# Row products dealt out between the sample tokens' selection operations, and U's blocks fetched three ahead of V in the last stage

## The reference, cut to what matters

```python
q = (xt @ w_q)                               # 8 heads, two halves of 128
s1, s2 = (halves of q against 128 sub-keys each)
v1, i1 = top_k(s1, 16);  v2, i2 = top_k(s2, 16)
cand = v1[:, None] + v2[None, :]             # 16 x 16 pairs a head
top_s, pos = top_k(cand, 16);  idx = i1 * 128 + i2 at pos
g = softmax(top_s)
act = gelu(u_tab[idx] . x)                   # 128 experts a token
out = sum(g * act * v_tab[idx])              # tables of 16384 x 1024
```

## Time and profile before

| | us |
|---|---|
| median of three timed runs | 2609.61 (2608.39 to 2610.11) |
| profiled execution, its own time | 2614.08 |
| its span, first to last instruction | 2612.3 |
| PE busy | 2377.7 (91% of the span) |
| DVE busy | 1766.5 (68%) |
| POOL busy | 908.3 (35%) |
| ACT busy | 777.9 (30%) |

### The profile page before, as it was taken

How to read it: one execution, slowest core, us unless ns; L and a number is a source line. 1 busy time by engine, 2 the same in 40 slices (tenths; PEclk the granted TensorE clock), 3 DMA queues, 4 the chain that set the end, 5 groups by cost and what they waited for, 6 DMA issues and landing times.

```text
span 2612.3 us, 34126 instructions
## 1 busy us (share of the span) xinstructions
PE 2377.7 (91%) x12686; PEld 1830.0 (70%) x12686; DVE 1766.5 (68%) x3612; ACT 777.9 (30%) x1388; POOL 908.3 (35%) x650
## 2 busy tenths in 40 slices
PE   5988899969999999999978778998899999999995
PEld 4756689859757766666657567987795777666662
DVE  1345479978668777677754456897884886777775
ACT  2354442113225422122243444311231452222221
POOL 3400360431221154555444205217113114555552
PEclk7999989989999999999989888999899999999997
DMA  6455334886799899999934702279669998999993
GB/s 262 139 179 193 131 112 129 312 313 226 281 316 317 281 366 370 366 364 366 366 115 147 209 25 85 92 269 360 207 223 344 313 320 316 377 378 356 384 369 133
DMA packets 219907, 679.71 MB, mean 260 GB/s; under 512 B 32384, under 2 KB 63152, under 8 KB 219232
## 3 DMA queue, kind: packets, MB, share of 16 engines
q1 hardware_dynamic: 142912, 396.42, 43.2%
q0 software_dynamic: 76832, 281.11, 28.7%
HBM read 658.87 MB, written 18.56 MB: 259 GB/s over the span
## 4 chain that ended last, share of the span: by engine, by line
PE 60%; DVE 15%; DMA 13%; ACT 4%; issue 3%; POOL 3%; SPq 1%; ACTq 0%; DVEq 0%
PE ps L1056 15%; PE ps L737 9%; PE ps L739 9%; PE ps L738 9%; DMA ring<-in_u 8%; PE ps L1033 7%; DVE arena L2033 3%; POOL arena L655 3%; PE ps L1012 2%; PE ps L919 2%; DMA arena<-gelu_half 2%; DMA arena<-in_u_rows,arena 2%; PE ps L900 2%; DVE arena L1927 1%; ACT u_split L1324 1%
## 5 line engine op out<-in xcount | busy, mean ns | idle before, releaser
L1056 PE MATMUL ps<-ring,arena 128*128 128x512 f32 x1264 | 568.9, 595 | 20.7 <-DVE arena L1981 20.6
L655 POOL DMA_INDIRECT arena<-in_u_rows,arena x256 | 294.0, 1148 | 782.6 <-DVE arena L2014 598.3
L655 POOL DMA_INDIRECT arena<-in_v,arena x256 | 355.8, 1390 | 353.8 <-DVE arena L2014 168.3
L1033 PE MATMUL ps<-arena,ring 128*128 128x256 f32 x2048 | 457.6, 382 | 1.1 <-ACT arena L1279 0.6
L1033 PEld LDWEIGHTS ps<-arena,ring 128*128 128x128 f32 x2048 | 386.5, 191 | 53.2 <-issue 1.9
L1056 PEld LDWEIGHTS ps<-ring,arena 128*128 128x128 f32 x1264 | 231.4, 190 | 268.8 <-issue 268.2
L615 POOL TENSOR_TENSOR ring_lo<-ring,ring_hi 128x1024 fp32r<-128x1024 f32 x84 | 216.4, 2588 | 415.5 <-ACT ring_hi L1158 415.5
L2014 DVE CUSTOM_DVE_ANT_0 arena<-arena 128x1024 f32<-128x1024 f32 x256 | 310.8, 1221 | 47.9 <-DMA arena<-in_u_rows,arena 47.5
L2033 DVE SCALAR_TENSOR_TENSOR arena<-arena 128x1024 f32<-128x1024 f32 x254 | 325.7, 1282 | 15.3 <-DMA arena<-in_v,arena 1.2
L737 PE MATMUL ps<-xs_high,u_split 128*128 128x256 f32 x1024 | 335.4, 328 | 0.1
L2003 DVE TENSOR_TENSOR u_split<-ring,u_split 128x1024 fp32r<-128x1024 f32 x128 | 156.7, 1224 | 218.4 <-ACT u_split L1324 218.4
(11 more groups left out here) (245 smaller groups left out, 3549.1 us busy)
## 6 DMA issues: line engine op xcount, KB each, us to landing
ring<-in_u SPq DMA_DIRECT2D x256, 512.0 KB, 6.3
ring<-in_v SPq DMA_DIRECT2D x256, 512.0 KB, 5.9
ring<-in_w_mod SPq DMA_DIRECT2D x80, 512.0 KB, 4.2
ring<-in_w_in SPq DMA_DIRECT2D x36, 512.0 KB, 3.3
ring<-in_w_q SPq DMA_DIRECT2D x32, 512.0 KB, 3.2
gelu_half<-arena SPq DMA_DIRECT2D x120, 128.0 KB, 4.7
arena<-gelu_half SPq DMA_DIRECT2D x120, 128.0 KB, 4.7
arena<-in_w_mod SPq DMA_DIRECT2D x16, 512.0 KB, 19.8
```

The costliest lines, as they stand in the source:

```text
L655: pool.indirect_dma_start(row[at], None, table, bass.IndirectOffsetOnAxis(where[:, k:k + 1], axis=0)).then_inc(sem(f"row_in{at}"), 16)
L1033: ins = mm(hidden_bank(b), slot[c % RING][:, P * k:P * k + P], HFS[:, k, :], start=(k == 0), stop=(k == KC - 1))
L1056: ins = mm(ps[:, t + 3 * q, :], GL[:, b % GLS, P * t - P:P * t], slot[c % RING][:, 512 * q:512 * q + 512], start=(b == MIDDLE[0]), stop=(b ...
```

## The change

```diff
-PICKED = 26
-PLAIN = 36
+PICKED = 37
+PLAIN = 39
-EARLY_DOTS = FIRST_DOTS + 20
-MIDDLE_DOTS = 38
+EARLY_DOTS = FIRST_DOTS + 16
+MIDDLE_DOTS = 42
...
         def u_chunk(l, b):
-            return c0 + b if b < SPILL else c0 + 128 + b - SPILL if b < SPILL + 2 else c0 + 130 + 2 * (b - SPILL - 2)
+            return c0 + b if b < SPILL else c0 + 128 + b - SPILL if b < SPILL + 3 else c0 + 131 + 2 * (b - SPILL - 3)
         def v_chunk(l, b):
-            return c0 + SPILL + (b + GLS) % SPILL if b < SPILL else min(c0 + 131 + 2 * (b - SPILL), c0 + KEYS + b)
+            return c0 + SPILL + (b + GLS) % SPILL if b < SPILL else min(c0 + 132 + 2 * (b - SPILL), c0 + KEYS + b)
...
-                    if b == 20:
+                    if b == 28:
                         exponents(1, P, STOK)
...
             def retrieve(l):
+                first_dots = iter(range(FIRST_DOTS))
+                def next_dot():
+                    for k in first_dots:
+                        dot(l, k)
+                        return True
...
-                def top16(pieces):
+                def top16(pieces, beside=False):
                     for s, v, x in pieces:
                         ins = dve.max(v[:, 0:8], s)
                     link(ins)
-                    for s, v, x in pieces:
+                    for n, (s, v, x) in enumerate(pieces):
                         ins = dve.max_index(x[:, 0:8], v[:, 0:8], s)
+                        if beside and n % 4 == 3:
+                            next_dot()
...
                     top16([(C[:, t, h, 0:CANDS], TV[:, t, h, :], TP[:, t, h, :])
-                           for t in range(first, last) for h in range(HEADS)])
+                           for t in range(first, last) for h in range(HEADS)], first > 0)
...
+                            if t:
+                                next_dot()
...
                 gates(1, 1, NT, ar(Q_ID + 7 * P, STOK)).then_inc(sem("picked"), 1)
+                while next_dot():
+                    pass
...
-                dots = 0
-                while dots < FIRST_DOTS:
-                    dot(dots)
-                    dots += 1
+                dots = FIRST_DOTS
```

More of the change, by code:

```diff
@@ L1833, in attention, with row_in, dot @@
                         mod_columns(MOD_STAGES[mods[0]][0] + (mods[1] + 2 * n - 6) // 4)
-            def retrieve(l):
+            def row_in(l, r):
+                n = PLACE[r]
+                dve.wait_ge(sem(f"row_in{row_slot[n]}"), 16 * row_turn(l, n))
+                return row[row_slot[n]]
+            def dot(l, k):
+                x = row_in(l, k)
+                dve.tensor_tensor_reduce(x, x, HP, 1.0, 0.0, ALU.mult, ALU.add,
+                                         HSEL[:, k:k + 1]).then_inc(sem("row_used"), 1)
+            def retrieve(l):
+                first_dots = iter(range(FIRST_DOTS))
[3 more added lines that the diff above has]
+                        return True
                 S = ar(Q_S, NT * 2048).rearrange("p (t c n) -> p t c n", t=NT, c=16)
@@ L2003, in low_u @@
                     tt(u_half(b, 1), slot[c % RING], f32(u_half(b, 0)), ALU.subtract).then_inc(used(c % RING), 1)
[L2005 to L2015, removed]
                 def dots_done(r):
@@ L2028, in accumulate @@
                 def accumulate(k):
-                    x = row_in(P + k)
+                    x = row_in(l, P + k)
                     if k:
@@ L2046, in experts @@
                     while dots < FIRST_DOTS + (EARLY_DOTS - FIRST_DOTS) * p // (PIECES - 1):
-                        dot(dots)
+                        dot(l, dots)
                         dots += 1
@@ L2079, in experts @@
                     for k in late_dots:
-                        dot(k)
+                        dot(l, k)
                     for k in late_sums:
```

## The result

The changed kernel takes 2546.3 us (median of four runs, 2539.5 to 2547.9) where the kernel before, run beside it, takes 2609.0: a ratio of 0.976, 95% interval 0.974 to 0.978, 62.7 us less. The forecast was 2560, its range 2538 to 2580. The profiled execution after is the fastest of the four, and that of before lay above its median, so the two profiles differ by more, 74.6 us of span. I therefore read the gain stage by stage. Here is the page of the changed kernel: the span and the groups of the two lines of PE that the change aimed at (busy us, mean ns, then the idle time in front and what ended most of it).

The account below looks back on a forecast made before the run. PE works nearly all of the mixer, so only its standing still could give time back. -32.6 + 2 - 19 = -49.6 took 2614.1 to 2564.5, less 4.5 to the median: 2560 us, range 2538 to 2580.

Parts of the forecast that it names:

- The hidden stage: Both layers' hidden stages: dealing products into the selection and picking later gives -32.6 us, bounds -22 to -50.
- U late from 486 to 537: Hidden stage beside dense gathers: 51 us in which 12.2 blocks of U arrive where PE could do 14.8.
- A starvation of 8.8 us a layer: Hidden stage: PE loses 8.8 us waiting for U beside the gathers, bounds 0 and 14.
- The first build at 563.6: Hidden stage: first one-hot build moves from 569.1 to 554.8 without new waits, to 563.6 with U late.
- the 127.6 us: Hidden stage behind the first build: 32 builds and 27 blocks in the old trace; 117.2 with three blocks moved ahead.
- The last stage: Last stages: U requested one pace of 6.30 us earlier removes PE's waits, -19 us, bounds 0 and -24.
- One of my marks: Last stage: sign to look for in the changed profile, U landing no sooner than now.
- The middle stage: Middle stages: four more products a layer cost +2 us, bounds 0 and 9.2 for both layers.
- rival 1: Hidden stage: U is not starved beside the gathers, gaining 17.6 us more, 2542 us; chance 0.17.
- Rival 2: Last stage is bound by bytes, giving back 17 of the 19 us, 2577 us; chance 0.15.
- Rival 3: Hidden stage: late rows push `picked` past block 37 and PE waits; 10 us a layer, 2580 us; chance 0.06.
- Rival 4: Last stage: V behind U(b + 3) in SP's queue, late in all 128 steps; at 0.5 us each, 2643; chance 0.05.

Follow-up runs that it names:

- e5: Changed kernel with only the first quarter of each of U's blocks 12 to 45 fetched in the hidden stage (computes something else); 2525.4 us, ratio 0.969.
- e2: Changed kernel with U fetched two ahead again, leaving only the products' part of the change; 2570.3 us, ratio 0.987 to the kernel before.
- e7: Changed kernel with 20 products among the builds and 38 in the middle stage instead of 16 and 42; 2538.5 us, ratio 0.975.
- e1: Kernel before with only U fetched three ahead; 2575.1 us, ratio 0.989.

## Why the prediction was right, and where it was off

**The hidden stage: -32.6 predicted, -35.6 in the profiles.** Its steps held to within a microsecond or two; in each pair here the first number is the prediction's. `picked` at 532.4: 532.55. The last product at 543.8: 543.9. U late from 486 to 537 at 4.17 us a block: from 487 to 533, mostly at 4.09 (491.82 to 495.91) and at 4.19 on average (eleven blocks from 487.13 to 533.23). A starvation of 8.8 us a layer: e5, which lifts it, gives 8.8 and 9.0. The first build at 563.6: 561.66, after a start that was 1.8 us earlier. The order of the queues was told rightly as well: U comes after 12.8 us where it was asked for 10.4 ahead. The missing 1.6 and 1.4 us a layer lie behind the first build. There I took the 127.6 us from the trace of before unchanged. But PE began them straight after a wait: this is the kernel before at the end of the wait, at the first build and after it (window, PE and PEld busy, DVE, ACT, POOL, granted clock, DMA share, GB/s).

```profile
541.00:569.00 28.00, 3.94 (x18) 2.96 (x16) 20.35 (x35) 0.77 (x2) 7.80 (x8) 0.63 0.90 361
569.00:571.00 2.00, 1.89 (x17) 1.89 (x18) 2.00 (x5) 0.00 (x0) 0.00 (x0) 0.50 0.00 0
571.00:575.00 4.00, 4.00 (x19) 3.41 (x19) 4.00 (x7) 1.08 (x2) 0.00 (x0) 0.88 0.00 0
```

The changed kernel at its first build:

```profile
560.00:566.00 6.00, 6.00 (x41) 5.37 (x40) 3.14 (x5) 1.47 (x3) 0.00 (x0) 1.00 0.60 199
```

Before, the granted clock is 0.50, 1.2 GHz, on the first build, which took 1.93 us there and 1.16 in the changed kernel, where it is 1.00; around the block behind it, it is 0.88 (4.22 against 3.67 us). So 1.3 of the 127.6 us, which I used for both layers, went with the wait. In layer 1 of the kernel before the same two took 1.93 and 5.58 us, 2.7 more than in the changed kernel.

**The last stage: -19 predicted, -29.7 measured.** This is the term of the sum that was mis-sized, and most of the 13.7 us between the forecast and the median. I set the gain nearly equal to the 20.7 us of listed waits and the bound at -24, which the measurement passes. The stage's whole length says more. Layer 0's last stage in the kernel before:

```profile
902.00:1314.00 412.00, 400.09 (x1978) 273.45 (x1978) 290.81 (x320) 85.73 (x127) 208.13 (x155) 1.00 0.95 356
```

and in the changed kernel:

```profile
876.00:1271.00 395.00, 395.00 (x1980) 272.67 (x1979) 293.26 (x321) 83.11 (x127) 208.32 (x155) 1.00 0.97 371
```

PE's busy time for the same instructions fell by 5.1 us, beside 11.9 us of listed waits: 17.0 of the 17.3. Most of it is not the clock, which has a mean of 1.00 in both. One wait of e2 tells it closely. It is listed as 0.97 us, but the `outer` behind it starts 1.13 us later than at the matmuls' pitch of 0.12 us, because the last matmul in front counts as busy for 0.28 us, to its end. The step from that `outer` to the next then takes 6.38 us and not 6.31. That makes 0.23 us beyond the list, about 5.5 us if all 24 waits are like it.

Another 1.7 us is the clock after all, in a stretch too short to show in the mean. It stands behind the longest wait of layer 0 in the kernel before (a row of PE's timeline, then a window as above):

```profile
1120.18 5.37 PE L1056 MATMUL ps<-ring,arena 128*128 128x512 f32 x8 [2.74 <-DVE arena L1981]
...
1121.60:1124.90 3.30, 3.30 (x5) 1.33 (x4) 3.20 (x4) 0.77 (x1) 2.34 (x3) 0.50 0.89 278
```

With the granted clock at 0.50 for most of it, the eight matmuls took 5.37 us and not 3.60, and the step to the next `outer` 8.07. e2 shows the same behind its longest wait, 3.0 us. What is left, some 1.8 us, was not read further.

The other readings of that stage hold: no wait for V appears at three ahead, and the bytes were no bound. The changed kernel's transfers from 902 to 1247 us:

```profile
DMA packets 36571, 133.90 MB, mean 388 GB/s; under 512 B 4062, under 2 KB 4062, under 8 KB 36421
...
ring<-in_v SPq DMA_DIRECT2D x56, 512.0 KB, 5.7
ring<-in_u SPq DMA_DIRECT2D x54, 512.0 KB, 7.4
```

Against the earlier trace rows the rate rose with the pace. The Trainium skill ("DMA: Bandwidth & Descriptors", section "Where 436 GB/s comes from") has the memory's limit for one core, near 358 GB/s, as what binds such transfers. By that rule the sum would have lacked the 19 us; 388 GB/s over 345 us and 415 over 50 us say that it doesn't bind here. One of my marks was wrong in sign: U was to land no sooner than before, and it lands in 7.4 us against 8.2.

**The middle stage: +2 predicted.** Not seen; e7 puts it at nothing.

**The rivals.** The median, 2546.3, lies closer to rival 1's 2542 than to my 2560, yet rival 1 (U not starved) is refuted by e5. A time near a rival's number does not speak for its mechanism: here two terms of the sum, 3.0 and 10.7 us too small, fill the gap. The forecast's own range, 2548 to 2572, was missed by 1.7 us; the median lies in the stated range because that took in rival 1. Rival 2 falls with e1. Rival 3 came near only with four buffers, and then at the products behind `picked`, not at `picked`. Rival 4 needs U four ahead, and then costs 6.3 us; its price of one delay in each of 128 steps was wrong.

## What to carry to other kernels

Price a set of short waits by the length of the stage against its pace without waits, not by the column of idle time: here waits of 0.2 to 3 us cost about half as much again as was listed. Moving work ahead of a point and moving that point back belong together and have to be tried together (alone they gained 8 and lost 4 us a layer, together they gained 18). Where gathers share the DMA engines with a stream that has a deadline, the number of gather buffers is a dial: too many starve the stream, too few starve the consumer, and the best lay at five or six where there were ten.

## What the runs showed that I had not expected

The number of gathers that can be under way changes how the DMA engines' time is split. Over the same 50 us, ten buffers gave the gathers 12.32 MB and SP's queue 8.37, five gave 9.97 and 9.40; U's landing time went from 12.8 to 6.9 us. The total fell only from 415 to 388 GB/s, and the kernel became some 10 us faster with fewer bytes a second.

The five executions with five buffers lie within 2.2 us of each other, those of the changed kernel's second series within 12.2. The buffers need not be the reason: with six they lie within 10.3 us, with four within 8.3. Why was not tried.
